# Turning the prompt's attention probabilities on VectorE and through DRAM instead of on TensorE, in one core of a decoder layer

## The chip, the core and the metric

The kernel runs on one core of a Trainium2 chip. It is one program written by hand for each engine: TensorE (PE), VectorE (DVE), ScalarE (ACT), GpSimd (POOL) and SyncE (SP), with semaphores between them. The metric is the device time of one execution in microseconds (us); a lower time is better. The rows quoted here come from one profiled execution of the kernel before.

## What is computed

One layer of a hybrid decoder over 512 prompt tokens and 8x4 sample tokens, all in float32: a norm, one wide input projection, an attention mixer with three branches, a gated mixer beside it, their projections, a merge and a last norm. What the change touches is the prompt's attention over selected and over window keys. With 512 tokens both branches see all keys up to the query's own position:

```
s = jnp.einsum('bqgjd,bkgd->bgjqk', q5, kw)
p = masked_softmax(s, mw[None, None, None])
o_win = jnp.einsum('bgjqk,bkgd->bqgjd', p.astype(vw.dtype), vw)
...
o = g[..., 0:1] * o_cmp + g[..., 1:2] * o_sel + g[..., 2:3] * o_win
```

There are 8 heads, as 2 key groups `g` of 4 heads `j`, each 64 wide. For the product with the values, the probabilities must stand with the keys on the partitions, while the softmax leaves them with the queries on the partitions. They have to be turned in between.

## The kernel before

`plan()` writes one list, `ORDER`, of steps. Every engine walks that same list and issues its own part of each step, so the list sets the order of the work on every engine. A step waits only where an engine's part has a semaphore wait in it. The steps `("main", ...)` are the blocks of the large projections: 24 matmuls of 128x272 each (line 1629), whose weights are split by ACT (`split`, line 951) and DVE (`low`, line 1214) from what SP loads. They need nothing of the attention and are laid between its steps, so that PE has work while the other engines do softmax; ACT reads each block's result out of its PSUM bank (line 1032), and there are two such banks.

The prompt's attention is cut into 16 units: four query tiles `i` of 128 tokens, times two branches `y`, times two halves `jh` of the heads. A unit of tile `i` holds four matrices (two heads by two groups) of 128 queries by 128(i+1) keys. Its steps are:

- `ps`, twice: PE scores (line 1936), DVE adds the mask and takes the maximum out of one of three PSUM banks (line 1524).
- `px`: ACT takes four exponentials with their sums (line 1122).
- `pn`: DVE makes the weights from sum and gate and scales the four matrices (line 1540).
- `pt`, once for each block of 128 keys: PE turns four 128x128 matrices (line 1943), and DVE or ACT by turns copies the result from PSUM to one of four places in SBUF (lines 1511 and 1115).
- `pp`, once for each block: PE multiplies by the values and adds into the bank `O` (line 1950).

`ct` and `cv` (lines 1916 and 1923) are the same two things for the small compressed branch, and `oz` folds `O` into `za` after each tile (line 1545). `AFTER_SCORES` says how many projection blocks follow each unit's scores; in all, 24 of them lie between the first scores and the last `oz`. After that come `zs` (lines 1132 and 1550) and the next projections, P0 to P3. The probabilities of two units fit at a time (`pb`); the tiles run from the narrowest (i = 0) to the widest (i = 3).

Of the kernel before, what the change touches and what calls it, by code (L numbers as in the profile page):

```python
# [158 lines left out]
AFTER_FIRST_SCORES, AFTER_SCORES, BEFORE_LAST_PRODUCTS = 2, [1, 1, 1, 1, 3, 1, 1, 1, 1, 1, 1, 1, 1, 1, 2, 2], 3  # L159
# [12 lines left out]
def plan():  # L172
# [120 lines left out]
    units = [(i, y, jh) for i in range(NT) for y in range(2) for jh in range(2)]  # L293
    limit = 35 + 8 + 16 + 16 + 10
    pending = []

    def products(keep):
        while len(pending) > keep:
            order.append(pending.pop(0))

    def turn_unit(u):
        for kt in range(units[u][0] + 1):
            order.append(("pt", u, kt))
            pending.append(("pp", u, kt))
            products(2)

    order += [("cx", 0)]
    for u, (i, g, y) in enumerate(units):
        n = u % 4
        order += [("ps", u, 0)]  # L310
        if u:
            order += [("pn", u - 1)]
            main(min(1, limit - state["n"]))
            order += [("ps", u, 1)]
            main(min(AFTER_SCORES[u] - 1, limit - state["n"]))
        else:
# [3 lines left out]
        if n == 1:  # L320
            order += [("cv", i, 0), ("cv", i, 1)]
        if u:
            turn_unit(u - 1)
        if n == 0:
            order += [("ct", i, 0), ("ct", i, 1)]
        order += [("px", u)]
        if n == 0:
            products(0)
            order += [("oz", i - 1)] if i else []
        if i < NT - 1 and n:  # L330
            order += [(("cs", "cx", "cn")[n - 1], i + 1)]
    order += [("pn", len(units) - 1)]
    main(min(BEFORE_LAST_PRODUCTS, limit - state["n"]))
    turn_unit(len(units) - 1)
    products(0)
# [42 lines left out]
def t_uses(s):  # L378
# [16 lines left out]
    if kind == "pt":  # L395
        return ["act" if (s[1] + s[2]) % 2 else "dve"]
# [15 lines left out]
PT_AT = {}  # L412
for _s in ORDER:
    if _s[0] in ("ct", "pt"):
        PT_AT[_s] = len(PT_AT)
NPT = 4
# [53 lines left out]
def nsa_gmlp_layer(nc, x_p, x_s, ck_cmp, cv_cmp, ck_sel, cv_sel, ck_win, cv_win, pages, w_in, w1k, w1v, w_sp,  # L470
# [4 lines left out]
    with ctx:  # L475
# [13 lines left out]
        cst = sb("cst", [P, NC_CONST])  # L489
        prm = sb("prm", [P, N_PARAM])  # L490
        wsT = sb("wsT", [P, 4, P])
# [71 lines left out]
        pb = U[:, 0:4096].rearrange("p (b j k) -> p b j k", b=2, j=J)  # L563
        ptb = U[:, 4096:6144].rearrange("p (r n) -> p r n", r=NPT)
# [4 lines left out]
        def sig_at(b, d):  # L569
# [26 lines left out]
        pads_zero, st_ready, mix_fn, pv_part, pt_used = (sem("pads_zero"), sem("st_ready"), sem("mix_fn"), sem("pv_part"),  # L596
                                                         sem("pt_used"))
# [106 lines left out]
        def _(sp):  # L704
# [43 lines left out]
            for s in ORDER:  # L748
# [10 lines left out]
                elif s[0] == "xt" and s[2] == 0 and s[1] % 5 in (1, 3):  # L759
# [4 lines left out]
                    n_win += 1  # L764
                elif s[0] == "oz" and s[1] == NT - 1:

                    sp.wait_ge(pt_used, len(PT_AT))
# [25 lines left out]
        def _(pool):  # L793
# [40 lines left out]
            def load(n):  # L834
# [3 lines left out]
                slot, done = ring[:, n % RING, :], ring_loaded[n % RING]  # L838
                if b == "p":
                    pool.wait_ge(cmp_out, 32)  # L840
                    src = (pk_cmp if w == "kc" else pv_cmp).rearrange("(m o r) c -> o m (r c)", o=2, r=8)
                    for o in range(2):
                        pool.dma_start(slot[32 * o:32 * o + 32, :], src[o, :, :]).then_inc(done, 16)
                else:
                    src = {"kc": ck_cmp, "vc": cv_cmp}[w]
                    pool.indirect_dma_start(slot, None, src, bass.IndirectOffsetOnAxis(cmp_rows[:, b:b + 1], 0)).then_inc(done, 16)

            def load_key(n):
                _, q, c, b = KEYS[n]
                pool.wait_ge(t_done, key_freed(n))  # L850
                slot, done = key_ring[:, n % KEY_RING, :], key_loaded[n % KEY_RING]
                b += QB * q
                if c == 2:
                    pool.dma_start(slot, ck_win[b].rearrange("(m r) c -> m (r c)", r=4)).then_inc(done, 16)
                else:
                    pool.indirect_dma_start(slot, None, ck_sel.rearrange("a (h c) -> (a h) c", h=2),
# [15 lines left out]
            for s in ORDER:  # L872
# [1140 lines left out]
```

## Time and profile before

| what | value |
|---|---|
| median of 3 runs | 620.76 us (620.16 to 623.88) |
| profiled execution, whole | 622.7 us |
| its span, first to last instruction | 621.0 us |
| PE busy | 585.7 us, 94% |
| DVE busy | 344.1 us, 55% |
| ACT busy | 248.2 us, 40% |
| POOL busy | 77.1 us, 12% |
| mean DMA rate | 113 GB/s |

A busy time is the union of an engine's instructions, whose recorded durations overlap on PE: what a PE instruction costs is read from the distance between two starts, not from its duration. In the timeline "x4" is four instructions of one kind in a row. PE multiplies float32 in more than one instruction for each operand pair, so one `pp` step is four rows of line 1950 and one `pt` step four of line 1943.

### The profile page before, as it was taken

The numbers are of one execution on the slowest core, as the hardware profiler recorded it, in microseconds if no ns is written. First come the engines' busy times: TensorE is split into PE (matmuls) and PEld (weight loads), VectorE is DVE, ScalarE is ACT, GpSimd is POOL, SyncE is SP. The second block draws the span as 40 slices with busy tenths as digits, with TensorE's granted clock in tenths as the row PEclk, the third lists the DMA queues.
The fourth block names the chain that finished last, engine by engine and source line by source line (L and its number), as shares of the span: only waits on it lengthen the run. The fifth ranks groups of instructions, "written<-read, shape, count | busy, mean of one in ns | idle before, by whom it ended". The sixth has DMA issues, their size and how long they took to land.

```text
span 621.0 us, 12850 instructions
## 1 busy us (share of the span) xinstructions
PE 585.7 (94%) x5262; PEld 519.9 (84%) x5262; DVE 344.1 (55%) x846; ACT 248.2 (40%) x557; POOL 77.1 (12%) x129
## 2 busy tenths in 40 slices
PE   7899999999899999988999999999999999997993
PEld 5899999999788997977888887666577899997992
DVE  5632213787687653353373756767655457762265
ACT  5543345447133434332331544435453352231333
POOL 0025431121011124504200000000000000000000
PEclk9999999999889999989999999999999999998998
DMA  9347723351353244924521220201111423306103
GB/s 309 136 139 231 237 69 135 137 193 62 103 170 135 72 136 137 334 73 148 225 84 55 68 69 2 69 1 35 35 34 35 143 70 103 102 2 237 35 2 144
DMA packets 45709, 70.02 MB, mean 113 GB/s; under 512 B 4178, under 2 KB 36114, under 8 KB 45395
## 3 DMA queue, kind: packets, MB, share of 16 engines
q1 hardware_dynamic: 38016, 44.85, 22.7%
q0 software_dynamic: 6912, 23.24, 11.0%
q10 hardware_dynamic: 722, 1.12, 0.5%
q8 instruction: 42, 0.69, 0.4%
q14 instruction: 17, 0.13, 0.1%
HBM read 65.23 MB, written 8.13 MB: 118 GB/s over the span
## 4 chain that ended last, share of the span: by engine, by line
PE 66%; DVE 8%; issue 2%; ACT 2%; DMA 1%; SPq 0%; ACTq 0%; DVEq 0%
PE m L1629 39%; PE s L1936 4%; PE o L1950 4%; PE t L1943 3%; PE s L1811 2%; PE s L1812 2%; PE s L1814 2%; PE t L1775 2%; PE t L1838 1%; DVE w_lo L1214 1%; PE o L1897 1%; DMA U<-in_x_p 1%; PE s L1790 1%; DVE xt_sb L1369 1%; PE s L1852 1%
## 5 line engine op out<-in xcount | busy, mean ns | idle before, releaser
L1629 PE MATMUL m<-h_hi,w_hi 128*128 128x272 f32 x448 | 134.6, 300 | 0.5 <-DVE w_lo L1214 0.5
L1629 PE MATMUL m<-h_hi,w_lo 128*128 128x272 f32 x448 | 129.8, 290 | 0.0
L1629 PE MATMUL m<-h_lo,w_hi 128*128 128x272 f32 x448 | 129.5, 289 | 0.0
L1629 PE MATMUL m<-w_hi,h_hi 128*128 128x256 f32 (+2 forms) x360 | 105.5, 293 | 4.2 <-DVE U L1577 2.0
L1629 PE MATMUL m<-w_hi,h_lo 128*128 128x256 f32 (+2 forms) x360 | 102.9, 286 | 0.0
L1629 PE MATMUL m<-w_lo,h_hi 128*128 128x256 f32 (+2 forms) x360 | 102.9, 286 | 0.0
L1629 PEld LDWEIGHTS m<-h_hi,w_hi 128*128 128x128 f32 x448 | 84.9, 190 | 10.6 <-issue 8.0
L1214 DVE TENSOR_TENSOR w_lo<-raw,w_hi 128x1024 fp32r<-128x1024 f32 (+2 forms) x62 | 71.1, 1154 | 35.3 <-ACT w_hi L951 35.2
L1629 PEld LDWEIGHTS m<-h_lo,w_hi 128*128 128x128 f32 x448 | 85.2, 190 | 0.0
L1629 PEld LDWEIGHTS m<-h_hi,w_lo 128*128 128x128 f32 x448 | 85.1, 190 | 0.0
L1629 PEld LDWEIGHTS m<-w_hi,h_hi 128*128 128x128 f32 (+1 forms) x360 | 68.8, 191 | 5.9 <-DVE U L1577 2.3
L1629 PEld LDWEIGHTS m<-w_lo,h_hi 128*128 128x128 f32 (+1 forms) x360 | 69.1, 192 | 0.1
L1629 PEld LDWEIGHTS m<-w_hi,h_lo 128*128 128x128 f32 (+1 forms) x360 | 68.9, 191 | 0.1
L951 ACT CAST w_hi<-raw 128x1024 fp32r<-128x1024 f32 (+2 forms) x62 | 61.0, 990 | 0.4 <-DMA raw<-in_w_in 0.4
L1369 DVE TENSOR_TENSOR xt_sb<-t,xt_sb 64x512 fp32r<-64x512 f32 x64 | 44.1, 689 | 9.9 <-PE s L1814 5.1
L1066 ACT CAST xt_sb<-t 64x512 fp32r<-64x512 f32 x56 | 32.5, 581 | 37.2 <-PE t L1775 36.0
L1032 ACT ACTIVATE U<-m 128x272 f32<-128x272 f32 x32 | 12.7, 397 | 71.4 <-PE m L1629 71.4
L1524 DVE CUSTOM_DVE_ANT_0 U<-s,cst 128x128 f32<-128x128 f32 (+3 forms) x64 | 28.8, 487 | 18.8 <-PE s L1936 18.7
L1629 PE MATMUL m<-x_hi,w_lo 128*128 128x272 f32 x128 | 36.8, 288 | 0.0
L1629 PE MATMUL m<-x_hi,w_hi 128*128 128x272 f32 x128 | 36.8, 287 | 0.0
L1629 PE MATMUL m<-x_lo,w_hi 128*128 128x272 f32 x128 | 36.8, 287 | 0.0
L1122 ACT ACTIVATE U<-U,st 128x128 f32<-128x128 f32 (+3 forms) x64 | 35.1, 552 | 1.4 <-DVE st L1528 1.4
(294 smaller groups left out, 968.1 us busy)
## 6 DMA issues: line engine op xcount, KB each, us to landing
raw<-in_w_in SPq DMA_DIRECT2D x36, 512.0 KB, 3.6
U<-in_x_p SPq DMA_DIRECT2D x8, 512.0 KB, 7.0
raw<-in_w_o SPq DMA_DIRECT2D x8, 512.0 KB, 3.9
raw<-in_w_in SPq DMA_DIRECT2D x8, 256.0 KB, 3.3
U<-in_ck_win POOLq DMA_DIRECT2D x8, 256.0 KB, 3.4
U<-in_cv_win POOLq DMA_DIRECT2D x8, 256.0 KB, 6.2
raw<-in_w_pa SPq DMA_DIRECT2D x8, 256.0 KB, 4.1
raw<-in_w_pb SPq DMA_DIRECT2D x4, 512.0 KB, 3.3
```

What stands on the lines that cost most here:

```text
L951: ins = nc.scalar.copy(hi, x)
L1032: nc.scalar.activation(sig_at(int(name[1] == "B"), d)[:, s[3] * HALF:(s[3] + 1) * HALF], m[:, 0:HALF], ACT.Tanh, scale=0.5).then_inc(main_ ...
L1066: ins = nc.scalar.copy(turned(xt_hi, r, g, b), TB[t % 2][64 * g:64 * g + 64, :].rearrange("p (q o n) -> p q o n", q=4, o=2))
L1122: ins = nc.scalar.activation(pb[:, u % 2, j, 0:n], pb[:, u % 2, j, 0:n], ACT.Exp, bias=st[:, m + 4 + j:m + 5 + j], scale=SCALE, accum_out= ...
L1214: ins = v.tensor_tensor(lo, x, hi.bitcast(F32), ALU.subtract)
L1369: ins = v.tensor_tensor(turned(xt_lo, r, g, b), TB[(t + m - n) % 2][64 * g:64 * g + 64, :].rearrange("p (q o n) -> p q o n", q=4, o=2), tu ...
L1524: v.tensor_tensor_reduce(pb[:, u % 2, a, 0:n], S[k % 3][:, 0:n], cs("causal")[:, 512 - n:512], 1.0, -3e38, ALU.add, ALU.max, st[:, m + a:m ...
L1629: ins = mm(out, lhs(a, k), rhs(b, k), start=(k == 0 and a + b == 0), stop=(k == n - 1 and a == 1))
L1775: ins = pe.transpose(tb[:, q * P:(q + 1) * P], x[:, (2 * q + r) * P:(2 * q + r + 1) * P], ident)
L1936: mm(S[k % 3][:, 0:n], qT[r, 2 * jh + jj, tok(i)], kT[r, y, 0:n], start=True, stop=True).then_inc(p_scored, 1)
L1943: ins = pe.transpose(tb[:, (2 * g + jj) * P:(2 * g + jj + 1) * P], pb[:, u % 2, a, kt * P:(kt + 1) * P], ident)
L1950: ins = mm(O[64 * g:64 * g + 64, 256 * jh:256 * jh + 256], v_tok[:, y, k, g * DH:(g + 1) * DH], ptb[:, PT_AT[("pt", u, k)] % NPT, 256 * g: ...
```

## The change

PE no longer turns the probabilities: the `pt` steps are gone. Instead:

- In `pn` ACT scales the four matrices, and DVE only makes the weights.
- A new step `tt`, one slot later, turns the unit on DVE in 32x32 blocks into one buffer `p_turn`; SP writes that buffer to DRAM in four DMAs of 32 partitions each (runs of 512 bytes), and POOL reads it back with one DMA (runs of 2 KB) over the unit's own slot. Written so, the blocks land where a full turn would have put them.
- There are four slots for units in place of two. The fourth lies over small attention buffers, and `p_turn` over parameters, that are no longer used by then.
- `pp` of a unit comes three units later (`LAG`), all blocks in a row, and its moving operand is read as eight runs of 32 elements.
- The tiles run from the widest to the narrowest, and `AFTER_SCORES` is another table. The number of projection blocks between the first scores and the last `oz` is still 24.

```diff
+TILES = (3, 2, 1, 0)
+LAG = 3
+AFTER_FIRST_SCORES, AFTER_SCORES = 2, [1, 2, 2, 2, 1, 1, 2, 1, 1, 1, 1, 1, 1, 1, 1, 0]
+LAST_TURN = (0, 1, 2)
...
+                elif s[0] == "tt":
+                    u = s[1]
+                    nb = 4 * (UNITS[u][0] + 1)
+                    sp.wait_ge(p_turned, u + 1)
+                    for a in range(4):
+                        sp.dma_start(p_dram[u, 0:nb, :, a * P:(a + 1) * P].rearrange("b j r -> j b r"),
+                                     p_turn[32 * a:32 * a + 32, 0:nb * P].rearrange("j (b r) -> j b r", b=nb)).then_inc(p_written, 16)
...
+                elif s[0] == "tt":
+                    u = s[1]
+                    i = UNITS[u][0]
+                    pool.wait_ge(p_written, 64 * (u + 1))
+                    pool.dma_start(slot[u % 4][:, 0:512 * (i + 1)].rearrange("p (k n) -> p k n", k=i + 1),
+                                   p_dram[u, 0:4 * (i + 1), :, :].rearrange("(k b) j n -> (b j) k n", b=4)).then_inc(p_moved[u % 4], 16)
...
+                elif kind == "pn":
+                    u = s[1]
+                    n = (UNITS[u][0] + 1) * P
+                    act.wait_ge(p_weight, u + 1)
+                    m = 80 + 20 * (u % 2)
+                    for j in range(J):
+                        ins = nc.scalar.activation(pb[u % 4][:, j, 0:n], pb[u % 4][:, j, 0:n], ACT.Copy, scale=st[:, m + 12 + j:m + 13 + j])
+                    ins.then_inc(p_scaled, 1)
...
                     if jj == 0:
-                        if u < 2:
+                        if u < 4:
                             dve.wait_ge(o_done, NQ)
                         else:
-                            dve.wait_ge(t_done, T_AT[("pt", u - 2, UNITS[u - 2][0])] + 1)
+                            dve.wait_ge(p_used, u - 3)
...
-                    for j in range(J):
-                        ins = v.tensor_scalar(pb[:, u % 2, j, 0:n], pb[:, u % 2, j, 0:n], st[:, m + 12 + j:m + 13 + j], None, ALU.mult)
-                    ins.then_inc(p_scaled, 1)
+                    v.tensor_tensor(w, w, gy, ALU.mult).then_inc(p_weight, 1)
+                elif kind == "tt":
+                    u = s[1]
+                    nb = 4 * (UNITS[u][0] + 1)
+                    dve.wait_ge(p_scaled, u + 1)
+                    dve.wait_ge(p_written, 64 * u)
+                    for j in range(J):
+                        dst = p_turn[:, 0:nb * P].rearrange("p (b j r) -> p b j r", b=nb, j=J)[:, :, j, :]
+                        ins = v.transpose(dst, pb[u % 4][:, j, 0:32 * nb].rearrange("p (b r) -> p b r", b=nb))
+                    ins.then_inc(p_turned, 1)
...
                 elif kind == "pp":
...
-                    wait_evacuated(pe, T_AT[("pt", u, k)])
+                    if k == 0:
+                        pe.wait_ge(p_moved[u % 4], 16 * (u // 4 + 1))
                     for g in range(G):
-                        ins = mm(O[64 * g:64 * g + 64, 256 * jh:256 * jh + 256], v_tok[:, y, k, g * DH:(g + 1) * DH],
-                                 ptb[:, PT_AT[("pt", u, k)] % NPT, 256 * g:256 * g + 256],
+                        ins = mm(O[64 * g:64 * g + 64, 256 * jh:256 * jh + 256].rearrange("p (j a r) -> p j a r", j=2, a=4),
+                                 v_tok[:, y, k, g * DH:(g + 1) * DH], p_blocks[u % 4][:, k, :, :, g, :].rearrange("p a j r -> p j a r"),
                                  start=False, stop=(y == 1 and k == i), skip_group_check=True)
```

What PE does in the kernel before behind the last unit's scores and two projection blocks: lines 1943 and 1950, turn and product, by turns.

```order
L1943 MATMUL t<-cst,U 128x128 [waits p_scaled,t_dve]
L1943 MATMUL t<-cst,U 128x128 x3
L1950 MATMUL o<-U,v_tok 64x256 [waits t_dve]
L1950 MATMUL o<-U,v_tok 64x256
L1943 MATMUL t<-cst,U 128x128 [waits t_act]
```

PE at the end of the attention in the changed kernel: the last unit's second scores (line 1956), the compressed products (1943), the products of units 12, 13 and 14 (1963), and then projection blocks (1649), behind two of which comes unit 15's product.

```order
L1956 MATMUL s<-kT,qT 128x128 [waits p_masked] x2
L1943 MATMUL o<-prm,vcp 64x512 [waits t_dve,mix_ready]
L1943 MATMUL o<-tmp,vcp 64x512 [waits t_act]
L1963 MATMUL o<-U,v_tok 64x256 [waits p_moved0]
L1963 MATMUL o<-U,v_tok 64x256
L1963 MATMUL o<-U,v_tok 64x256 [waits p_moved1]
L1963 MATMUL o<-U,v_tok 64x256
L1963 MATMUL o<-U,v_tok 64x256 [waits p_moved2]
L1963 MATMUL o<-U,v_tok 64x256
L1649 MATMUL m<-h_hi,w_hi 128x272 [waits lo_done,main_act]
```

The turns are gone, and each unit's product waits on a semaphore of the DMA that POOL posts. On DVE the same place read as follows before, with the copies (line 1511) out of PSUM behind the last scores:

```order
L1528 TENSOR_SCALAR st<-st 128x4 [waits p_masked]
L1511 COPY U<-t 128x512 [waits pt_used,t_done] x2
L1535 RECIPROCAL st<-st 128x4 [waits p_exp]
L1538 TENSOR_TENSOR st<-st,gate 128x4 [waits dve_step]
L1540 TENSOR_SCALAR U<-U,st 128x512 [waits dve_step]
L1540 TENSOR_SCALAR U<-U,st 128x512 x3
L1214 TENSOR_TENSOR w_lo<-raw,w_hi 128x4x256 [waits hi_done]
```

And in the changed kernel, where the turns of units 14 and 15 (line 1560) both lie behind the last scores:

```order
L1543 TENSOR_SCALAR st<-st 128x4 [waits p_masked]
L1560 STREAM_TRANSPOSE p_turn<-U 128x4x32 [waits p_written,p_scaled]
L1560 STREAM_TRANSPOSE p_turn<-U 128x4x32 x3
L1549 RECIPROCAL st<-st 128x4 [waits p_exp]
L1552 TENSOR_TENSOR st<-st,gate 128x4 [waits dve_step]
L1560 STREAM_TRANSPOSE p_turn<-p_slot 128x4x32 [waits p_written,p_scaled]
L1560 STREAM_TRANSPOSE p_turn<-p_slot 128x4x32 x3
L1231 TENSOR_TENSOR w_lo<-raw,w_hi 128x4x256 [waits hi_done]
```

The scaling has left DVE, the turns stand there, and each of them waits until the write of the unit before it has landed.

## Rows read from the trace of the kernel before

**Rows 1.** The page: engines' busy time over the span, share, instructions.

```profile
PE 585.7 (94%) x5262; PEld 519.9 (84%) x5262; DVE 344.1 (55%) x846; ACT 248.2 (40%) x557; POOL 77.1 (12%) x129
```

**Rows 2.** Windows (us from start): busy us (instructions) by engine, PEclk, DMA share, GB/s.

```profile
330.40:488.00 157.60, 156.56 (x1100) 115.29 (x1100) 97.80 (x314) 70.50 (x191) 0.00 (x0) 1.00 0.14 41
...
164.00:167.00 3.00, 2.15 (x16) 2.18 (x17) 1.78 (x5) 0.00 (x0) 0.00 (x0) 0.87 0.05 12
167.00:176.00 9.00, 9.00 (x46) 8.56 (x46) 4.14 (x9) 0.31 (x1) 0.00 (x0) 0.50 0.00 0
```

**Rows 3.** Timeline of PE in a narrow tile: start, us, instruction, count.

```profile
351.67 0.49 PE L1936 MATMUL s<-kT,qT 64*128 64x128 f32 x4
352.09 0.66 PE L1943 MATMUL t<-cst,U 128*128 128x128 f32 x4
...
353.10 0.40 PE L1629 MATMUL m<-h_hi,w_hi 128*128 128x272 f32 x1
...
356.33 0.49 PE L1936 MATMUL s<-kT,qT 64*128 64x128 f32 x4
```

**Rows 4.** Timeline of PE, widest tile: blocks turned and multiplied by turns.

```profile
460.59 0.66 PE L1943 MATMUL t<-cst,U 128*128 128x128 f32 x4
461.18 0.65 PE L1950 MATMUL o<-U,v_tok 128*64 128x256 f32 x4
461.76 0.66 PE L1943 MATMUL t<-cst,U 128*128 128x128 f32 x4
...
462.93 1.13 PE L1936 MATMUL s<-kT,qT 64*128 64x512 f32 x4
463.99 0.39 PE L1629 MATMUL m<-h_hi,w_hi 128*128 128x272 f32 x1
```

**Rows 5.** Timeline of PE: compressed probabilities turned, then two products in a row.

```profile
437.73 1.06 PE L1916 MATMUL t<-cst,U 128*31 128x128 f32 x8
438.72 1.08 PE L1950 MATMUL o<-U,v_tok 128*64 128x256 f32 x8
439.74 1.13 PE L1936 MATMUL s<-kT,qT 64*128 64x512 f32 x4
```

**Rows 6.** Group of PE, 330.4 to 488: busy us, mean ns, idle before and releaser.

```profile
L1943 PE MATMUL t<-cst,U 128*128 128x128 f32 x160 | 25.3, 284 | 0.7 <-DVE U L1511 0.7
```

**Rows 7.** Groups of DVE in the same window.

```profile
L1524 DVE CUSTOM_DVE_ANT_0 U<-s,cst 128x128 f32<-128x128 f32 (+3 forms) x64 | 28.8, 487 | 18.8 <-PE s L1936 18.7
L1540 DVE TENSOR_SCALAR U<-U,st 128x128 f32<-128x128 f32 (+3 forms) x64 | 20.4, 382 | 0.6
L1511 DVE COPY U<-t 128x512 f32<-128x512 f32 (+1 forms) x24 | 16.5, 689 | 23.3 <-PE t L1943 16.1 <-PE t L1916 7.0
```

**Rows 8.** Groups of ACT in the same window.

```profile
L1122 ACT ACTIVATE U<-U,st 128x128 f32<-128x128 f32 (+3 forms) x64 | 35.1, 552 | 1.4 <-DVE st L1528 1.4
L1115 ACT COPY U<-t 128x512 f32<-128x512 f32 (+1 forms) x24 | 14.0, 584 | 26.9 <-PE t L1943 22.6 <-PE t L1916 4.1
```

**Rows 9.** Timeline of ACT: the first exponential of one 128-wide unit.

```profile
357.60 0.40 ACT L1122 ACTIVATE U<-U,st 128x128 f32<-128x128 f32 x1 [0.77 <-DVE st L1528]
```

**Rows 10.** Timeline of DVE: the two masks that follow a 128-wide score step.

```profile
353.31 0.29 DVE L1524 CUSTOM_DVE_ANT_0 U<-s,cst 128x128 f32<-128x128 f32 x1 [0.40 <-PE s L1936]
```

**Rows 11.** Line 770, four posts of 32 partitions: ns min/median/max to post one.

```profile
L770 SPq DMA_DIRECT2D U<-in_x_s x4: 597/609/1431, 488.1 to 490.9; - x4
```

**Rows 12.** DMA issues of the whole run: KB each, median us to landing.

```profile
raw<-in_w_in SPq DMA_DIRECT2D x8, 256.0 KB, 3.3
U<-in_ck_win POOLq DMA_DIRECT2D x8, 256.0 KB, 3.4
...
out_pk_cmp<-U POOLq DMA_DIRECT2D x1, 256.0 KB, 2.9
...
U<-in_x_s SPq DMA_DIRECT2D x4, 32.0 KB, 2.2
```

**Rows 13.** DMA queues in 216 to 222: two loads of 512-byte runs on q1.

```profile
q1 hardware_dynamic: 1056, 0.52, 33.7%
```

More of the change, by code:

```diff
@@ L292, in plan, with products @@
     assert 59 <= state["n"] <= 61
-    units = [(i, y, jh) for i in range(NT) for y in range(2) for jh in range(2)]
+    units = [(i, y, jh) for i in TILES for y in range(2) for jh in range(2)]
     limit = 35 + 8 + 16 + 16 + 10
[L295 to L305, printed above, removed]
+    def products(u):
+        order.extend(("pp", u, kt) for kt in range(units[u][0] + 1))
     order += [("cx", 0)]
-    for u, (i, g, y) in enumerate(units):
-        n = u % 4
+    for u in range(len(units)):
+        n, k = u % 4, u // 4
         order += [("ps", u, 0)]
@@ L315, in plan @@
             main(min(AFTER_SCORES[u] - 1, limit - state["n"]))
+            order += [("tt", u - 1)]
         else:
@@ L319, in plan @@
             main(min(AFTER_SCORES[u], limit - state["n"]))
[L320 to L323, printed above, removed]
         if n == 0:
-            order += [("ct", i, 0), ("ct", i, 1)]
+            order += [("ct", k, 0), ("ct", k, 1)]
         order += [("px", u)]
[L327 to L335, printed above, removed]
+        if n == LAG:
+            order += [("cv", k, 0), ("cv", k, 1)]
+        if u >= LAG:
+            products(u - LAG)
+        if n == LAG - 1 and k:
+            order += [("oz", k - 1)]
+        if k < NT - 1 and n:
+            order += [(("cs", "cx", "cn")[n - 1], k + 1)]
+    last = len(units) - 1
+    order += [("pn", last), ("tt", last)]
+    for n in range(LAG):
+        products(last - LAG + 1 + n) if n < LAG - 1 else None
+        main(min(LAST_TURN[n], limit - state["n"]))
+    products(last)
     order += [("oz", NT - 1)]
@@ L595, in nsa_gmlp_layer @@
         rows_ready, ws_masked, rope_step = sem("rows_ready"), sem("ws_masked"), sem("rope_step")
-        pads_zero, st_ready, mix_fn, pv_part, pt_used = (sem("pads_zero"), sem("st_ready"), sem("mix_fn"), sem("pv_part"),
-                                                         sem("pt_used"))
+        pads_zero, st_ready, mix_fn, pv_part = sem("pads_zero"), sem("st_ready"), sem("mix_fn"), sem("pv_part")
+        p_weight, p_turned, p_written, p_used, c_used = sem("p_weight"), sem("p_turned"), sem("p_written"), sem("p_used"), sem("c_used")
+        p_moved = [sem(f"p_moved{n}") for n in range(4)]
         ssq_ready, root_in, root_done, h_ready = sem("ssq_ready"), sem("root_in"), sem("root_done"), sem("h_ready")
@@ L1108, in _ @@
                     nc.scalar.activation(cp, cp, ACT.Exp, scale=SCALE).then_inc(c_exp, 1)
-                elif kind in ("ct", "pt") and T_AT[s] < len(T_USE) and t_uses(s) == ["act"]:
+                elif kind == "ct" and t_uses(s) == ["act"]:
                     act.wait_ge(t_done, t + 1)
-                    r = PT_AT[s]
-                    if r >= NPT:
-                        act.wait_ge(pt_used, r - NPT + 1)
-                    rows = NCP if kind == "ct" else P
-                    nc.scalar.copy(ptb[0:rows, r % NPT, :], TB[t % 2][0:rows, :]).then_inc(t_act, 1)
+                    if s[1]:
+                        act.wait_ge(c_used, G * s[1])
+                    nc.scalar.copy(ctb[s[2]][0:NCP, :], TB[t % 2][0:NCP, :]).then_inc(t_act, 1)
                 elif kind == "px":
@@ L1504, in _ @@
                     v.tensor_tensor(c3, c3, st[:, 16:24].unsqueeze(2).broadcast_to([P, H, NCP]), ALU.mult).then_inc(c_p, 1)
-                elif kind in ("ct", "pt") and t_uses(s) == ["dve"]:
+                elif kind == "ct" and t_uses(s) == ["dve"]:
                     dve.wait_ge(t_done, t + 1)
-                    r = PT_AT[s]
-                    if r >= NPT:
-                        dve.wait_ge(pt_used, r - NPT + 1)
-                    rows = NCP if kind == "ct" else P
-                    v.tensor_copy(ptb[0:rows, r % NPT, :], TB[t % 2][0:rows, :]).then_inc(t_dve, 1)
+                    if s[1]:
+                        dve.wait_ge(c_used, G * s[1])
+                    v.tensor_copy(ctb[s[2]][0:NCP, :], TB[t % 2][0:NCP, :]).then_inc(t_dve, 1)
                 elif kind == "ps":
```

82 lines of the change are left out of this document (36 added, 46 removed).

## The prediction

> **What bounds the kernel now.** The page comes first: PE is busy 94% of the span, DVE 55% and ACT 40% [rows 1]. The question is whether that holds in the stage that is changed. The windows answer it: from the first prompt scores (330.4) to the last `oz` (about 488), 157.6 us, PE is busy 156.6, DVE 97.8 and ACT 70.5, and the clock is granted in full [rows 2]. So the stage is as long as the list of PE's instructions, and a PE instruction taken out of it is worth its pitch (the distance between starts), if nothing else comes late. The groups say the same from the other side: before the turns PE waited 0.7 us for DVE in all [rows 6], while DVE's and ACT's idle time before their copies ends with PE [rows 7, 8]. The timelines then give the prices. A turn of one block costs 461.18 - 460.59 = 0.59, a product beside a turn 461.76 - 461.18 = 0.58 [rows 4]; two products in a row cost 439.74 - 438.72 = 1.02, or 0.51 each [rows 5]. A score step is 352.09 - 351.67 = 0.42 at 128 keys [rows 3] and 463.99 - 462.93 = 1.06 at 512 [rows 4], between them 0.63 and 0.85 by a straight line. A projection block is 356.33 - 353.10 = 3.23 [rows 3]. With 24 blocks (77.5), 32 score steps (23.7), 40 turns (23.4), 40 products (23.4) and about 10 for the compressed branch this is 158, the stage as measured.
>
> **What PE gives up.** There are 4 x (1+2+3+4) = 40 turns: 40 x 0.585 = 23.4 us. The products remain, but now stand in rows; of 40, the 24 that are not the first of their unit fall from 0.585 to 0.51: 1.8. PE's idle time in the stage is 157.6 - 156.6 = 1.0 [rows 2], and most of it is the wait for PSUM copies: 1.0. Sum 26.2. Against this stands the new form of the product's moving operand, eight runs of 32 in place of one of 256; no row has such runs. Below, its bound is nothing; above, the only spread that products show among themselves is 0.07 (0.51 against 0.58 [rows 4, 5]), 3 us over 40. I take nothing, since the count of columns is the same, and keep the 3 for the range.
>
> **What DVE and ACT take on.** DVE loses 64 scalings (20.4) and 20 of 24 copies (20 x 0.69 = 13.8) [rows 7]. It gains 64 turns by blocks, which no row shows: the nearest are the scaling, one operand in SBUF, 0.38 on the mean, and the copy from PSUM, 0.69 for 512 columns [rows 7], so 24 to 31 us by size. I take 28: DVE falls from 97.8 to about 92. ACT loses 20 copies (11.7) and gains 64 scalings, for which the exponentials without their read-out are the nearest row: 64 x 0.55 = 35 at most [rows 8], about 30. ACT rises from 70 to about 90 in a stage of some 135. Neither engine becomes the bound by its sum; the waits are what matters.
>
> **The round trip, and its first new wait: the one buffer.** `tt(u)` waits until unit u-1 is written. One cycle is then DVE's four turns, the write, and the wake-up. For the write: a post of 32 partitions takes SP 0.61, four of them 2.4, and the last lands 2.2 after its post when small [rows 11, 12]; 3 x 0.61 + 2.2 = 4.0 for the narrowest tile. For the widest, 2048 runs of 512 bytes: on the load of such runs 1056 packets took 33.7% of 16 engines in 6 us, that is 31 ns each [rows 13], so 2048 x 31 / 16 = 4.0, with 2.2 makes 6.2. A store of 256 KB in such runs landed in 2.9, a load in 3.3 [rows 12], so I see no sign that DRAM as the target is dearer. With turns of 2.4, 1.8, 1.4 and 1.1 the cycles are 8.6, 7.0, 5.6 and 5.1 from the widest tile to the narrowest. A slot of PE (two score steps, its projection blocks, its products) is 2 x 1.06 + 2 x 3.23 = 8.6 for the widest tile, 1.7 + 3.2 + 2.1 to 2.5 = 7.0 to 7.4 for the next, 1.3 + 3.2 + 1.0 to 1.6 = 5.5 to 6.1, and 0.8 + 3.2 + 1.0 = 5.1. They are equal: the buffer just keeps pace. DVE late by under 3 us stops nothing, since PE has a projection block between the two score steps and three score banks. I take 1 us of stalls in the middle, from 0 to 8.
>
> **The second wait: PE at the products.** `pp(u)` stands three slots behind its scores. For the widest tile: masks 1.3, exponentials behind the slot's last projection block, weights, scaling 2.5, turns 2.4, write 6.2, read. POOL's read of 256 KB in 2 KB runs lands in 3.4 [rows 12]; 1 MB, about 3.4 + 0.75 MB at the 267 GB/s that 31 ns for 512 bytes on 16 engines make, less for longer runs: 5.3 to 6.2. Counted slot by slot this ends 2 to 8 us before PE gets there, in the second and third tile 0.5 to 5 us before. **At the end it does not.** Units 14 and 15 have no slots behind them. Counted from the end of PE's last score step: PE does the compressed products (about 1.1, as the turns of the same size in [rows 5]) and units 12 and 13 (0.59 + 0.51), and is at unit 14 after 2.2. DVE masks 0.29 more and makes the bias, 0.6 in all [rows 10], turns unit 14 until 1.7; the write lands at 1.7 + 4.0 = 5.7, POOL wakes 0.3 later (an estimate; each of its waits in the trace ends so) and its read lands at 5.7 + 0.3 + 3.4 = 9.4. PE stands still for 9.4 - 2.2 = 7.2 us. With quicker posts and reads it would be 5, with slower ones 9. Unit 15: its exponentials (4 x 0.4, [rows 9]) and its scaling are over by then, but its turns wait for the write of unit 14, 5.7 to 6.8, then 10.8, then 14.5; PE has the two projection blocks and comes at 9.4 + 0.5 + 6.4 = 16.3. No second stall.
>
> **The clock.** Around 164 PE stood still for a few us, and the granted clock went to 0.50, its lower level of 1.2 GHz, and stayed there from 167 to 176 [rows 2]. A stall of 7 us may do the same here. Of work at the lower level half the time is lost; but what follows are dense projection blocks and no thin ones, so I take 1.5 us, from 0 to 4.
>
> **Sum.** -26.2 + 1 + 7.2 + 1.5 = -16.5. What lies behind `oz` (zs, P0) keeps its order and its distance. The profiled execution took 622.7, so it would be 606.2; the median of the runs is 620.76, 2 us less, and I forecast 604 for the median.
>
> **A page against the trace.** The Trainium skill, "DMA: Bandwidth & Descriptors" (section on completion latency and the fixed 2 us), says that the semaphore of a DMA fires only when the last byte is confirmed, and that this can be surprisingly long when the target is HBM. By it the writes would be dearer than the loads; the trace's stores and loads of 256 KB show 2.9 and 3.3, the other way round. The Trainium skill, "VectorE: DVE Perf Modes" (rules for kernel authors), advises TensorE for a 128x128 turn where PSUM will do as the target: a rule against this change. It names no price for the round trip; what it would mean here is the third rival.
>
> **Rivals.** (1) **The end is hidden**: if the chain of unit 14 is shorter than counted, or the stage's middle gives back what the end costs, only the sum on PE stays: 620.8 - 26 = 595. For it: PE bounds the stage everywhere; against: every term of the chain has a row. (2) **The waits are longer in the middle**: chains of ACT and DVE, each now in the other's path twice per unit, come late by half a microsecond to one per unit, or the short runs cost 3: 604 + 3 to 11, about 611. The equality of cycle and slot speaks for it. (3) **The buffer becomes the bound, and the kernel slower**: if a write of 512-byte runs to DRAM takes twice what the loads of such runs take (10.2, 8.2, 6.2, 5), the cycles are 12.6, 10, 7.6 and 6.1 against slots of 9, 7.3, 6 and 5.1 with four units each: 14 + 11 + 6 + 4 = 35, less the 3 that are covered: 604 + 31 = 635. It decides from 16.5 / 16, about 1 us that each cycle is longer than its slot. Against it: the store in [rows 12]. (4) **Nothing gained**: half of that, the cycles about 1 us too long, or the raw loads behind the writes on SP's queue coming late: 615 to 625.
>
> **How the numbers follow.** Forecast 0.52 (599 to 609); rival 1 0.15; rival 2 0.15; rival 4 0.10; rival 3 0.08. The range leaves out rival 3 and the upper half of rival 4: 594 to 618. Faster by over 1% (under 614.6; about what a measurement of this kernel can tell from no change): 0.52 + 0.15 + most of rival 2 = 0.80; within 1%: 0.11; slower: 0.09.
>
> **What would show it.** Right: no PE turns from U; the stage about 141 us long in place of 157.6; `pp` waiting for a DMA once, for unit 14, 5 to 9 us; DVE's waits for `p_written` short; SP posting four writes in about 2.4 us. Wrong: DVE's turns ending late in every slot after a wait for a write (rival 3), PE waiting for a DMA in every unit (rival 2), products with a pitch over 0.6, or no wait at the end at all (rival 1).

## The result, and the profile after

The changed kernel took 618.21 us (median of 17 runs, 614.35 to 622.58), the kernel before, run beside it, 621.78 (17 runs, 619.16 to 624.40): a ratio of 0.9944, with a 95% interval of 0.9921 to 0.9968. So it is faster by 0.6%, less than the 1% that counts as a change here, and 14 us slower than the forecast of 604, just outside the range of 594 to 618. The forecast had given 0.80 to a gain of over 1% and 0.11 to what came. PE's work fell as it should; the gain went to waits and to what came with them.

The page of the changed kernel: busy times, the granted clock and the DMA engines in 40 slices of the span, the chain that ended last by line, and landing times of the trip's DMAs. It answers to [rows 1, 12].

```profile
span 614.7 us, 12596 instructions
PE 565.3 (92%) x5102; PEld 506.0 (82%) x5102; DVE 335.5 (55%) x826; ACT 266.1 (43%) x601; POOL 88.6 (14%) x145
PEclk9999999999879999999999998999897999999998
...
DMA  8347822452334244842822177777685533307103
...
PE m L1649 29%; DMA p_dram<-p_turn 9%; DVE p_turn L1560 3%; SPq L768 3%; PE t L1858 1%; PE s L1831 1%; PE s L1832 1%; PE s L1834 1%; DMA U<-in_x_p 1%; PE t L1795 1%; PE o L1917 1%; DVE w_lo L1231 1%; DMA p_slot<-p_dram 1%; PE s L1872 1%; PE o L1963 1%
...
p_dram<-p_turn SPq DMA_DIRECT2D x16, 256.0 KB, 5.1
U<-p_dram POOLq DMA_DIRECT2D x3, 1024.0 KB, 6.3
```

The chain now runs through the write of the one buffer (9%) and the turns behind it. The windows give the stage from the first prompt scores to the last `oz` in the first row, then two stretches with a write alone (355 to 360) and with all transfers at once (370 to 380), and then the stretches where the clock fell; the columns after the window are its length, each engine's busy time, the clock, the DMA engines' share and their rate. The first row answers to [rows 2].

```profile
330.20:484.60 154.40, 140.07 (x943) 104.99 (x943) 88.98 (x294) 88.30 (x235) 11.07 (x16) 0.94 0.60 175
355.00:360.00 5.00, 5.00 (x36) 4.10 (x35) 3.47 (x13) 2.85 (x5) 0.00 (x0) 1.00 0.75 179
370.00:380.00 10.00, 8.20 (x58) 5.80 (x56) 6.62 (x20) 5.50 (x14) 0.76 (x1) 1.00 0.96 298
380.00:390.00 10.00, 8.66 (x50) 5.54 (x52) 5.31 (x15) 5.06 (x14) 0.75 (x1) 0.83 0.62 187
430.00:440.00 10.00, 8.14 (x51) 5.56 (x50) 7.57 (x28) 4.79 (x16) 0.71 (x2) 0.83 0.80 247
470.00:475.00 5.00, 1.70 (x8) 0.33 (x6) 0.89 (x4) 0.00 (x0) 0.54 (x1) 0.50 0.45 116
475.00:480.00 5.00, 5.00 (x25) 4.80 (x24) 0.00 (x0) 0.00 (x0) 0.54 (x1) 0.57 0.18 52
```

PE is busy for 140.1 us of the stage and idle for 14.3, and the clock is at 0.94 on the mean where it was 1.00. Counted in both kernels from the start of the first scores to the end of the last `oz`, the stage is 154.5 us long (330.2 to 484.7) where it was 158.0 (330.4 to 488.4); [rows 2] end at 488.0, inside that `oz`. Of the 6.3 us by which the span is shorter (621.0 to 614.7), 3.5 lie in the stage and 2.6 behind it: behind the last `oz` the two kernels have the same work, and it took 130.0 us in place of 132.6.

PE's timeline shows the waits. These are products of line 1963 (it answers to line 1950 in [rows 3 to 5]); x16 is a unit of the widest tile, the bracket the idle time before it. The last two are units 13 and 14.

```profile
370.05 1.95 PE L1963 MATMUL o<-U,v_tok 128*64 128x256 f32 x16
371.93 0.92 PE L1956 MATMUL s<-kT,qT 64*128 64x384 f32 x4
...
380.46 3.56 PE L1963 MATMUL o<-U,v_tok 128*64 128x256 f32 x16 [2.26 <-DMA U<-p_dram]
...
389.80 1.95 PE L1963 MATMUL o<-U,v_tok 128*64 128x256 f32 x16 [0.89 <-DMA U<-p_dram]
...
469.73 1.12 PE L1963 MATMUL o<-U,v_tok 128*64 128x256 f32 x4 [2.86 <-DMA U<-p_dram]
...
474.15 1.12 PE L1963 MATMUL o<-U,v_tok 128*64 128x256 f32 x4 [3.30 <-DMA U<-p_dram]
```

Unit 0's four steps took 371.93 - 370.05 = 1.88, or 0.47 each: the runs of 32 in the moving operand cost nothing. Unit 1 waited 2.26 us and then ran at 1.2 GHz, 3.56 in place of 1.95. In all PE waited for the trip 8 times, 13.9 us: 6 times in the middle for 7.7 and twice at the end for 6.2. It never waited for the weights of a projection block, so the loads that stand behind the writes on SP's queue were not late for it (rival 4's second half). DVE's turns show the one buffer (the bracket as above):

```profile
361.64 2.49 DVE L1560 STREAM_TRANSPOSE p_turn<-U 128x512 f32<-128x512 f32 x4 [2.72 <-DMA p_dram<-p_turn]
372.09 2.49 DVE L1560 STREAM_TRANSPOSE p_turn<-U 128x512 f32<-128x512 f32 x4 [1.39 <-DMA p_dram<-p_turn]
383.36 2.49 DVE L1560 STREAM_TRANSPOSE p_turn<-p_slot 128x512 f32<-128x512 f32 x4 [5.18 <-DMA p_dram<-p_turn]
393.35 1.96 DVE L1560 STREAM_TRANSPOSE p_turn<-U 128x384 f32<-128x384 f32 x4 [3.15 <-DMA p_dram<-p_turn]
```

The four starts are 10.5, 11.3 and 10.0 us apart, against a slot of 8.6 on PE. From the end of unit 2's turn (372.09 + 2.49 = 374.6) to the end of the wait for its write (383.36) lie 8.8 us, from unit 3's (385.85) to 393.35 7.5, and from unit 0's (351.87 + 2.48, first of its line) to 361.64 7.3. In all DVE waited 27.6 us for the write, 13 times.

### The profile page after: what moved, and what is told of

Read it like the earlier page. It is cut to its first block, busy times and chain, and to the rows that moved or that the text cites. A ratio compares the mean times of both kernels' runs of the same rounds, so it can differ in the third digit from the quotient of the medians.

```text
span 614.7 us, 12596 instructions
## 1 busy us (share of the span) xinstructions
PE 565.3 (92%) x5102; PEld 506.0 (82%) x5102; DVE 335.5 (55%) x826; ACT 266.1 (43%) x601; POOL 88.6 (14%) x145
## 4 chain that ended last, share of the span: by engine, by line
PE 41%; DMA 11%; DVE 9%; ACT 3%; SPq 3%; issue 2%; ACTq 0%; DVEq 0%
PE m L1649 29%; DMA p_dram<-p_turn 9%; DVE p_turn L1560 3%; SPq L768 3%; PE t L1858 1%; PE s L1831 1%; PE s L1832 1%; PE s L1834 1%; DMA U<-in_x_p 1%; PE t L1795 1%; PE o L1917 1%; DVE w_lo L1231 1%; DMA p_slot<-p_dram 1%; PE s L1872 1%; PE o L1963 1%
## 5 line engine op out<-in xcount | busy, mean ns | idle before, releaser
L1140 ACT ACTIVATE U<-U,st 128x512 f32<-128x512 f32 (+3 forms) x48 | 23.1, 551 | 25.2 <-DVE st L1552 25.2
L1831 PE MATMUL s<-xt_sb,w_hi 128*128 128x256 f32 x128 | 31.3, 286 | 1.7 <-DVE xt_sb L1379 1.2
L1832 PE MATMUL s<-xt_sb,w_lo 128*128 128x256 f32 x128 | 30.8, 282 | 0.0
```

The source lines that it names most:

```text
L1140: ins = nc.scalar.activation(pb[u % 4][:, j, 0:n], pb[u % 4][:, j, 0:n], ACT.Copy, scale=st[:, m + 12 + j:m + 13 + j])
L1831: mm(out[:, 0:256], w, xt_hi[:, x], start=(j == 0), stop=False, skip_group_check=True)
L1832: ins = mm(out[:, 0:256], w1_lo[:, j, :], xt_hi[:, x], start=False, stop=False, skip_group_check=True)
```

## The experiments

Each run's ratio is to the kernel before on the same chip, with its 95% interval. The changed kernel stands at 0.9944.

### Without the round trip

```diff
-                    for a in range(4):
-                        sp.dma_start(p_dram[u, ...], p_turn[32 * a:32 * a + 32, ...]).then_inc(p_written, 16)
...
-                    pool.dma_start(slot[u % 4][...], p_dram[u, ...]).then_inc(p_moved[u % 4], 16)
...
-                        pe.wait_ge(p_moved[u % 4], 16 * (u // 4 + 1))
+                        pe.wait_ge(p_turned, u + 1)
```

SP's, POOL's and DVE's waits that belong to the trip are gone with it, DVE's `dve.wait_ge(p_written, 64 * u)` too.

> The changed kernel without its round trip: no write to DRAM and no read back; the product waits only until DVE has turned the unit and reads the unturned probabilities in its slot, so the attention output is not the reference's. All of PE's, DVE's and ACT's instructions stay. My theory (PE's sum was right, and the gain of 26 was lost to waits for the trip and the clock they pull down): about 22 us under the changed kernel, 594 to 598, the stage 131 to 134 us with the clock at 1.00. Rival A (ACT's scaling and DVE's turns, each now in the other's chain, make PE wait too): 603 to 610, with PE waiting for p_turned. Rival B (the gain was never there, products with short runs are dearer): 612 or more.

593.89 us, ratio 0.957 (0.9527 to 0.9613), 0.1 us under the theory's lower edge and far from both rivals. A window over the stage:

```profile
330.20:460.70 130.50, 130.50 (x940) 100.54 (x939) 88.14 (x289) 88.84 (x235) 0.00 (x0) 1.00 0.16 46
```

PE is busy without a gap at the full clock. The first scores start at 329.4 here, before this window, so the stage is 131.3 us; the prediction's sum for PE alone was 157.6 - 26.2 = 131.4. ACT's scaling and DVE's turns stay in this kernel and delay nothing. The changed kernel's stage is 154.5 - 131.3 = 23.2 longer: 14.3 of idle time, and 8.9 that the same work took longer. Of these, about 6 are the lower clock, worked out from the rows above as busy time times what the clock lacks: 8.66 x 0.17 + 8.14 x 0.17 = 2.9 in the middle and 1.70 x 0.50 + 5.00 x 0.43 = 3.0 at the end. For the other 3 us no row gives a cause. All of it comes with the trip.

### Two buffers in turn

```diff
+        turn_at = [(U[:, 11776:13824] if len(UNITS) and UNITS[u][0] == 3 else U[:, 12288:13824]) if u % 2 and u < 8
+                   else p_turn[:, 1024 * (u % 2 if u >= 8 else 0):] for u in range(len(UNITS))]
...
-                    dve.wait_ge(p_written, 64 * u)
+                    if u > 1:
+                        dve.wait_ge(p_written[u % 2], 64 * (u // 2))
```

> Two turning buffers in turn instead of one, so DVE turns a unit without waiting for the write of the one before. My theory (one buffer with a write of 7 to 9 us in place of 6 sets the cycle, and PE's waits in the middle are its consequence): DVE's waits for a write fall from 27.6 to under 5 us, PE's waits in the middle from about 8 to under 3, and the lows of the clock at 380 and 430 go: 608 to 612. The end keeps its two waits. Rival A (the DMA engines are the bound: two writes, a read and the loads share them, so each gets longer): waits move from DVE to PE, 615 to 620. Rival B (ACT's late weights start the chain late, whatever the buffer): 615 to 618.

616.84 us, ratio 0.9943 (0.9911 to 0.9976): the same as with one buffer. My theory falls, rival A holds; rival B has the same figure, but without the trip ACT's late weights cost nothing. The waits of the stage (engine, line, for what; us in total, times, longest) and the landing of the widest reads:

```profile
PE o L1967 <- DMA U<-p_dram: 14.6, 6, 4.3
PE o L1967 <- DMA p_slot<-p_dram: 1.4, 2, 1.3
...
U<-p_dram POOLq DMA_DIRECT2D x3, 1024.0 KB, 9.4
```

No wait of DVE for a write is left, but the reads of the widest tile, which now have other writes and the weight loads beside them, land in 9.4 us in place of 6.3, and PE waits 16.0 in place of 13.9. The products came no sooner: the stage took 154.1 us (328.6 to 482.7) in place of 154.5.

### The end filled, and both edits together

```diff
     for n in range(LAG):
+        main(min(1, limit + 1 - state["n"]))
         products(last - LAG + 1 + n) if n < LAG - 1 else None
-        main(min(LAST_TURN[n], limit - state["n"]))
```

> One projection block is laid before each of the products of units 13, 14 and 15, one of them taken from behind the last mix (25 blocks in the stage in place of 24, no block added in all). My theory (at the end the lost time is 6.2 us of PE's waits and some 4 us of blocks at the lower clock behind them): the last mix falls at about 481 to 482 with one block more done, 6 to 9 us under the changed kernel, 609 to 613. Rival (the wait only moves behind the blocks, since unit 15's trip ends at 478 to 481 anyway, and the mix is then followed by too few blocks to cover the splits before P0): 614 to 618.

610.09 us, ratio 0.9814 (0.9777 to 0.9851), in the range of the theory. The last `oz` begins at 482.6, 1.4 earlier than at 484.0, though one block of 3.2 us more is done by then; the trace is of the slowest of the five runs (614.1 us), so it shows less of the gain than the median. The cost of the end is a cause of its own.

> Two buffers and the filled end together. My theory: the causes are separate and add up, 600 to 606, the stage near 135 to 139 us, clock about 1.00. Rival (traffic bound): 608 to 614.

610.9 us, ratio 0.982 (0.9776 to 0.9864): the rival's figure. The second buffer adds nothing to the filled end either.

### The writes in long runs, and from two queues

```diff
+                    rows = p_dram[u, 0:nb, :, :].rearrange("b j n -> (b j n)").rearrange("(a j n) -> a j n", a=4, j=32)
...
-                        sp.dma_start(p_dram[u, 0:nb, :, a * P:(a + 1) * P].rearrange("b j r -> j b r"),
-                                     p_turn[32 * a:32 * a + 32, 0:nb * P].rearrange("j (b r) -> j b r", b=nb)).then_inc(p_written, 16)
+                        sp.dma_start(rows[a], p_turn[32 * a:32 * a + 32, 0:nb * P]).then_inc(p_written, 16)
```

> The changed kernel with the same four writes of 32 partitions and the same bytes per unit, but each partition's row is written as one contiguous run (8 KB for the widest tile) in place of runs of 512 bytes; the read stays. The blocks land in other places than a turn would put them, so the attention output is not the reference's. After the two-buffer run (DVE's waits gone, PE's waits larger, time the same) my theory is that the DMA engines' time is what the trip costs, most of it in 2048 packets of 512 bytes. Then the widest unit's write falls from 7.3-8.8 us to 4-5.5, reads beside it get faster too, PE's waits for the trip fall from 14 to under 7 us: 606 to 611. Rival A (a write of 32 partitions is slow whatever its runs, as its four posts of 0.6 us or its target set it): cycles stay, 616 to 619. Rival B (latency of two transfers one behind the other, not their bytes): 613 to 617.

614.21 us, ratio 0.9887 (0.9860 to 0.9915): some 3.5 us, the figure of rival B, not of my theory (that the bytes do count is shown by the kernel with a small read, below). The whole run has 51594 packets in place of 70026. The first write took 6.2 us from the end of its turn in place of 7.3, and 4 to 5.5 were expected; DVE still waited 20.2 us for writes, and PE 11.5 for reads. So the 2048 packets of 512 bytes are a small part of the cost. In the second kernel SyncE posts `a` = 0 and 1 and GpSimd 2 and 3, on a semaphore of its own:

> The changed kernel, with two of each unit's four writes posted by SyncE and two by GpSimd, at the same time. My theory (the DMA engines' time sets the write): the widest write stays at 6.5 to 8.5 us, 616 to 620. Rival (posting one behind the other on one queue keeps a quarter of the engines idle during a write, 0.77 busy at 174 GB/s): the write falls to about 5.5 us, DVE's waits from 27.6 to under 15: 611 to 615.

618.47 us, ratio 0.9969 (0.9946 to 0.9992). DVE waited 29.9 us. Posting one behind the other is not what made the write slow.

### Only the order of the tiles

The kernel before, with `TILES = (3, 2, 1, 0)` in its plan, the indices that follow from it, and its own `AFTER_SCORES`.

> The kernel before, with its turns on TensorE, its two slots and its table of blocks, and only the tiles taken from the widest to the narrowest. My theory (the order carries no gain of its own, since TensorE bounds the stage in either order): 619 to 623, the same as before. Rival (the last unit's short chain before the last mix is worth something, and so a part of the changed kernel's 3.5 us comes from the order): 615 to 618. On the other side, DVE's masks and scalings of the widest tile come first, with little laid ahead: 624 to 628.

624.9 us, ratio 1.0065 (1.0034 to 1.0097): slower by 4 us. The last `oz` begins at 490.36, where it began at 487.74. The new order is no gain; with this table of blocks it costs some 4 us as long as PE does the turns. Whether the changed kernel, whose PE sum holds in that order, still pays it was not tried.

### The write alone, and a read of few bytes

The first kernel drops the read, and PE waits for `p_written`:

> The changed kernel without the read: the write to DRAM stays, with its one buffer, and the product waits for the write and takes the unturned probabilities that still lie in the slot, so the attention output is not the reference's. It halves the bytes of the trip and takes its second transfer (3 to 8 us) off each unit's chain, but leaves the one buffer. My theory now (what costs is the chain of two transfers per unit and their share of the DMA engines, together): DVE's waits for the write fall from 27.6 to about 20 us since the reads no longer run beside it, PE waits under 4 us, at the end only: 598 to 603. Rival (the one buffer's cycle alone sets the stage, as I first had it): still 610 or more.

601.57 us, ratio 0.9677 (0.9653 to 0.9701). DVE waited 14.9 us for writes, and PE 2.9 for the trip, once, at the end. A widest unit's write took 7.1 to 7.5 us from the end of its turn, so with a turn of 2.5 the cycle of the one buffer is 9.6 to 10 against a slot of 8.6, with no read anywhere; yet it stopped PE for 0.9 us only in the middle. The one buffer with its writes to DRAM is thus worth at most 601.6 - 593.9 = 8 us, and the read the other 17. What of this is bytes and what the step itself, the second kernel tells:

```diff
-                    pool.dma_start(slot[u % 4][:, 0:512 * (i + 1)].rearrange("p (k n) -> p k n", k=i + 1),
-                                   p_dram[u, 0:4 * (i + 1), :, :].rearrange("(k b) j n -> (b j) k n", b=4)).then_inc(p_moved[u % 4], 16)
+                    pool.dma_start(slot[u % 4][:, 0:P], p_dram[u, 0:4, :, 0:P].rearrange("b j n -> (b j) n")).then_inc(p_moved[u % 4], 16)
```

> The changed kernel with the whole chain of its trip (write, GpSimd's wait, read, product waiting for the read), but the read brings only 64 KB of each unit (1 MB for the widest) into its slot; the rest of the slot stays unturned, so the attention output is not the reference's. It keeps the read's place in the chain and takes away its bytes. Without any read the kernel took 601.6, with the whole one 618.2. Theory A (the read costs through its bytes: its own long landing and its share of the DMA engines beside the writes): 603 to 606, the small read landing in 2.2 to 2.6 us. Theory B (a second transfer in the chain costs, whatever its size): 609 to 614, with PE's waits at the middle products still 5 us or more.

605.39 us, ratio 0.9747 (0.9702 to 0.9791): theory A. Its waits in the stage, and the landing of the first three reads (over all 16 it is 2.2 to 2.7):

```profile
DVE p_turn L1559 <- DMA p_dram<-p_turn: 17.4, 9, 4.1
...
PE o L1962 <- DMA U<-p_dram: 5.2, 2, 3.2
...
U<-p_dram POOLq DMA_DIRECT2D x3, 64.0 KB, 2.2
```

Every wait of PE for the trip in the middle is gone; both that are left stand at the end, for units 13 and 14. Of the read's 16.6 us, 605.4 - 601.6 = 3.8 are the step and 12.8 its bytes: the time they take to land, and what they take from the writes and loads beside them. How the 12.8 divide between these two was not tried.

### Straight from SBUF to SBUF

If the bytes are the cost, half of them can go: the blocks are copied from the turning buffer into the slot without DRAM, in 16 DMAs per unit. SyncE posts `a` = 0 and 1 (shown) and GpSimd 2 and 3. This kernel has the two buffers and the filled end.

```diff
+                    for a in (0, 1):
+                        for b in range(4):
+                            sp.dma_start(slot[u % 4][32 * b:32 * b + 32, 0:512 * k].rearrange("p (k n) -> p k n", k=k)[:, :, a * P:(a + 1) * P],
+                                         turn_at[u][32 * a:32 * a + 32, 0:512 * k].rearrange("p (k n) -> p k n", k=k)[:, :, b * P:(b + 1) * P]).then_inc(p_written[u % 2], 16)
```

> As the kernel with both edits (two turning buffers, filled end), but the blocks move from the turning buffer into their slot directly, SBUF to SBUF, in 16 transfers of 32 partitions for each unit (8 posted by SyncE, 8 by GpSimd), with nothing written to DRAM and nothing read back. My theory (engines' time and the two transfers in a row are the cost): per widest unit 1 MB moved in place of 2, ready 5 to 9 us after the turn in place of 14 to 17; PE's waits for the trip under 3 us, the clock at 1.00 throughout: 595 to 600. Rival A (the posts, 8 of 0.6 us on each queue, become the bound in the narrow tiles, where a slot is 5.1 us, and hold back SyncE's loads of weights): 603 to 612. Rival B (16 transfers of small packets cost more engine time than they save): 610 to 620.

598.89 us, ratio 0.9652 (0.9623 to 0.9682), the fastest kernel here that does all the work. A window over its stage, and its first and last posts on SyncE's queue:

```profile
330.20:467.60 137.40, 134.13 (x964) 103.47 (x963) 89.49 (x287) 89.10 (x236) 67.10 (x128) 1.00 0.49 122
...
353.37 5.28 SPq L774 DMA_DIRECT2D U<-p_turn  x8
...
459.96 5.03 SPq L774 DMA_DIRECT2D p_slot<-p_turn  x8
```

From its first scores at 329.2 the stage is 138.4 us, with 25 projection blocks where there were 24, so for the same work it is 135.2. The clock is at 1.00 throughout, and PE waits 3.3 us for the trip, all at the end, where eight posts still take 5.0 us although the unit is a quarter of the size (rival A, but small).

With one buffer and the end as it was, the same transport does this:

> The changed kernel with only the transport replaced: 16 transfers from SBUF to SBUF per unit, half posted by SyncE and half by GpSimd, one turning buffer, the end as in the changed kernel. My theory (two transfers in a row and their bytes were the cost, and the second buffer is worth little): 602 to 606, DVE's waits for the buffer 10 to 25 us but PE's waits in the middle under 2, and 3 to 5 at the end. Rival (the direct kernel's gain needed the second buffer): 608 to 613.

629.96 us, ratio 1.0137 (1.0106 to 1.0167): slower than before. The rival had the direction, and neither had the size. Its stage and four of its turns:

```profile
330.20:496.30 166.10, 144.79 (x940) 107.56 (x939) 87.74 (x289) 87.59 (x235) 67.10 (x128) 0.93 0.39 100
...
429.62 1.42 DVE L1567 STREAM_TRANSPOSE p_turn<-U 128x256 f32<-128x256 f32 x4 [3.05 <-DMA p_slot<-p_turn]
437.52 1.43 DVE L1567 STREAM_TRANSPOSE p_turn<-U 128x256 f32<-128x256 f32 x4 [2.28 <-DMA U<-p_turn]
446.35 1.42 DVE L1567 STREAM_TRANSPOSE p_turn<-U 128x256 f32<-128x256 f32 x4 [4.96 <-DMA U<-p_turn]
454.26 1.42 DVE L1567 STREAM_TRANSPOSE p_turn<-p_slot 128x256 f32<-128x256 f32 x4 [3.70 <-DMA U<-p_turn]
```

In this tile the prediction's slot of PE is 5.5 to 6.1, and the turns are 7.9 to 8.8 apart: eight posts hold the buffer for 5.1 us whatever the unit's size, and the last lands after them. DVE waited 55.6 us for the buffer, late masks held PE's scores 8 times for 11.7 in all, and PE waited 9.6 at units 13 and 14. This is rival 3 of the prediction, by another cause. Between this kernel and the direct one lie two edits, the second buffer and the filled end, and 31 us; the filled end was worth 8 with the trip through DRAM. So with this transport the second buffer most likely counts for the most, but it alone was not tried.

The last kernel lets SyncE post 7 of 16 transfers in the two narrow tiles and gives the narrowest four buffers:

> As the direct kernel with two buffers and the filled end, but SyncE posts 7 of 16 transfers in the two narrow tiles (its posts took 0.63 us, GpSimd's 0.49), and the narrowest tile has four buffers, so its last turn doesn't wait 3.0 us. Theory (posts of 8 x 0.63 on SyncE against a slot of 5.1 cost the last three products 1.0 to 1.2 us each): PE's waits at the end fall from 3.3 to under 1.5 us, 595 to 598. Rival (the wait is the transfers' own latency): 598 to 600, as without it.

603.99 us, ratio 0.9707 (0.9673 to 0.9741): slower than without (0.9652), though the intervals just overlap. PE waited 5.0 us for unit 15, whose nine posts on GpSimd stood still between the first and the second:

```profile
457.63 0.50 POOL L931 DMA_DIRECT2D p_slot<-p_turn  x1
460.35 3.92 POOL L931 DMA_DIRECT2D p_slot<-p_turn  x8 [2.22 <-issue]
```

The first of these rows is GpSimd's 128th post of the trip. The direct kernel has 128 in all, and shows no such pause inside a unit.

## Why the prediction was wrong

**What bounds the kernel, and what PE gives up: right.** The sum for PE alone was 131.4 us, and without the trip the stage took 131.3. The products' pitch was 0.47 where I took 0.51, and the short runs cost nothing, as taken.

**What DVE and ACT take on: right.** DVE's turns took 20.3 + 6.8 = 27.1 us (64, in two groups) where I took 28, ACT's scalings 23.1 + 7.7 = 30.8 where I took 30. The stages' sums were 89.0 and 88.3, forecast 92 and 90, and neither holds anything up in the kernel without the trip.

**The end: right in size, split in two.** The wait was forecast as 7.2 at unit 14 alone; it was 2.86 at unit 13 and 3.30 at unit 14, 6.2 in all. The buffer was late by then, so unit 13 was late too.

**"The buffer just keeps pace" and "I take 1 us of stalls in the middle": this is the step that failed.** The middle's idle time was 14.3 - 6.2 = 8.1 us, at the upper bound that I gave and far from the 1 that I took. Two things under it were mis-sized. The write of the widest unit was priced at 6.2; it took 7.3 with nothing of the trip beside it (7.1 to 7.5 in the kernel without reads), and 7.5 to 8.8 beside a read. The store of 2.9 that I took as a sign that DRAM is no dearer a target is one of six of that size in the profile before, which landed in 2.8 to 3.8. More than that, each transfer was priced as if alone: 6.2 for the write and 5.3 to 6.2 for the read, while between 370 and 380 the write of one unit, the read of another and the weight loads share engines that are busy for 0.96 of the time at 298 GB/s. The Trainium skill, "DMA: Bandwidth & Descriptors" (Anatomy of one DMA), fits one DMA as 2.0 us plus its bytes at 436 GB/s; that estimate would be 4.4 us for the 1 MB read, and the trace does not agree: 6.3, and 9.4 in the kernel with two buffers. No read of ours stood alone, so the fit itself was not tried. The chain of a widest unit has a margin of 2 to 8 us by my count, and the second and third tile's of 0.5 to 5; those sums were made with the transfers alone, and that used them up. What shows the step is the kernel with a small read. It has my chain, my buffer and my writes, only not the read's bytes, and on PE it does what I forecast for the whole: waits for the trip at the end only (5.2), a stage of 141.6 us (329.9 to 471.5, forecast 141), 605.4 us (forecast 604). Its DVE still waited 17.4 us, where I had those waits short, and its cycles there are 9.5 to 10 us against a slot of 8.6: that the buffer keeps pace was wrong by itself too, but that cost PE only 1.1 us in the middle (two late masks) until the read's bytes came on top.

**Which resource it was I first had wrong too.** The trace reads as if the one buffer were it: DVE waited 27.6 us for it, and the chain that ended last runs through it. Two buffers took all of that away and gained nothing. DVE's wait was the place where the late transfers showed first: without it the writes began earlier, and the reads took longer to land (9.4 in place of 6.3). Rival 2 (longer waits in the middle, 611) had the place, but neither the cause (ACT's and DVE's chains, or the short runs) nor the size. Rival 4 (nothing gained, 615 to 625, chance 0.10) had the time, but in part by luck: its cycles came out too long, by 1.4 to 2.7 us in the widest tile, yet taking the buffer's wait away gained nothing, and its late weight loads never held PE.

**The clock: mis-sized.** Forecast 1.5 (0 to 4), measured about 6. I counted one fall, at the end, where the clock was at 0.50 from 470 to 475 and 0.57 to 480; it cost 3.0, inside my bounds. The stalls in the middle brought two more, at 380 and 430 (0.83 over 10 us each), for 2.9, and there I had counted nothing. Before the fall at 380 PE had stood still 2.26 us for unit 1, and had only scores and the compressed branch's turns to do before it. The Trainium skill, "TensorE: Matmul & The Clock Gate" (HAM oscillation), describes such a pattern, waits for a DMA between short stretches of matmul that bring the clock down again and again; the trace agrees with three falls, and I weighed it at one place only.

**The sum once more.** The stage was forecast at 141 and took 154.5, 13.5 more: 7.1 by the stalls in the middle, 4.4 by the clock and 3 by work that took longer without a cause that a row shows, for which I had no term, less 1.0 at the end.

**What lies behind `oz`** I took as unchanged; in the two profiles it was 2.6 us shorter (132.6 to 130.0). This is no effect of the change that the runs can show: the same work took 131.0 without the trip, 129.8 with two buffers, and 131.3 in the kernel before with only its order turned. The profiled execution of the changed kernel is also 1.7 us faster than its median, so the 6.3 us between the two spans overstate the 3.6 between the medians. Open is the write's own rate: alone, between 355 and 360, it ran at 179 GB/s with 0.75 of the engines' time busy; long runs changed the total by 3.5 us only, and a second queue by nothing.

## What to carry to other kernels

Price a transfer with all that moves beside it, not from a row in which it stood alone: add the bytes of a slot over the DMA engines and compare with the slot, as one does for a compute engine. A wait on a buffer proves that the buffer is late, not that a second one would help; and stalls of PE cost more than their length, here 8.9 us on top of 14.3, about 6 of them by the clock. When a turn through memory is the price, copy within SBUF, with two buffers and work laid in front of the last products: here 599 us, 3.5% under the kernel before, where the same turn through DRAM gave 0.6%, and 1.9% with the same filled end.

## What the runs showed of the hardware

- 64 turns by 32x32 blocks in float32, SBUF to SBUF, took DVE 27.1 us; four of 128x512 took 2.48.
- A float32 moving operand in runs of 32 elements cost PE nothing: 0.47 us per step in a row, where two steps with contiguous operands had 0.51.
- Writes of 1 MB from SBUF to DRAM in 512-byte runs, four DMAs of 32 partitions, took 7.3 us from the end of the turn with nothing of the trip beside them, and 7.1 to 7.5 in the kernel without reads; a read of 1 MB back in 2 KB runs landed in 6.3, and in 9.4 with two buffers; one of 64 KB in 2.2 to 2.7.
- A post on SyncE for a DMA of 32 partitions took 0.66 us for 64 KB and 0.63 for 16 KB (5.28 and 5.03 for eight), one on GpSimd 0.49 to 0.55.
- GpSimd stood still for 2.2 us between its 128th and 129th post of the trip, in the one kernel that has more than 128. What it waited for no row shows.
